# Expert pairs written out four times instead of looped; token positions moved from VectorE to GpSimd

## What is computed

```python
logits = h @ w_router
top_val, top_idx = lax.top_k(logits, 2)
top_w = jax.nn.softmax(top_val)
for e in range(8):
    out = out + gates[..., e:e + 1] * (silu(h @ w_gate[e]) * (h @ w_up[e])) @ w_down[e]
```

## Time and profile before

| | |
|---|---|
| median of 3 runs (lowest, highest) | 1273.4 us (1270.49, 1274.1) |
| the profiled execution's own time | 1276.08 us |
| its span in the trace | 1274.2 us |
| mean granted TensorE clock | 0.985 of full |
| TensorE busy | 1221.2 us, 96% of the span |
| VectorE busy | 689.5 us, 54% |
| ScalarE busy | 539.2 us, 42% |
| GpSimd busy | 106.9 us, 8% |
| DMA | 412.58 MB, mean 324 GB/s |

### The profile page before, as it was taken

The page is one execution under the profiler, slowest core; times in us unless marked ns, Lnnn a source line. Parts: engine busy times, 40 slices in busy tenths (PEclk is TensorE's granted clock), DMA queues, the critical chain, the costliest instruction groups (busy, mean ns, idle before and its releaser), DMA issues.

```text
span 1274.2 us, 16146 instructions
## 1 busy us (share of the span) xinstructions
PE 1221.2 (96%) x6044; PEld 854.6 (67%) x6044; DVE 689.5 (54%) x783; ACT 539.2 (42%) x522; POOL 106.9 (8%) x118
## 2 busy tenths in 40 slices
PE   9999999989989999998899999889999988999996
PEld 7888887778877888334688833568883346888332
DVE  3844445656578888102688710268861026886102
ACT  2643444455445776002577500257750025775001
POOL 0000000000003050100005010000501000050100
PEclk8999999999999999999999999999999999999998
DMA  9755553853266999999999999999999999999995
GB/s 314 257 187 178 196 178 120 199 188 131 100 248 225 372 363 360 347 409 414 413 415 406 368 371 408 415 414 415 407 346 386 407 415 414 415 406 341 391 407 209
DMA packets 141294, 412.58 MB, mean 324 GB/s; under 512 B 9683, under 2 KB 29139, under 8 KB 141142
## 3 DMA queue, kind: packets, MB, share of 16 engines
q1 hardware_dynamic: 140406, 408.23, 84.5%
q0 software_dynamic: 816, 3.28, 0.8%
HBM read 410.44 MB, written 1.05 MB: 323 GB/s over the span
## 4 chain that ended last, share of the span: by engine, by line
PE 85%; DMA 5%; DVE 3%; SPq 3%; issue 3%; ACT 1%; DVEq 0%; ACTq 0%
PE bank L1395 19%; PE bank L1396 19%; PE bank L1397 19%; PE bank L1768 13%; DMA raw<-in_moe_w_gate 4%; PE bank L1781 4%; SPq L545 3%; PE bank L1721 1%; PE bank L1402 1%; PE bank L1844 1%; PE bank L1491 1%; PE bank L1798 1%; PE bank L1657 1%; DMA head_row<-in_heads 1%; ACT w_hi L604 1%
## 5 line engine op out<-in xcount | busy, mean ns | idle before, releaser
L906 DVE TENSOR_TENSOR raw_lo<-raw,w_hi 128x2048 fp32r<-128x2048 f32 x149 | 339.8, 2300 | 101.4 <-ACT w_hi L604 101.2
L604 ACT ACTIVATE w_hi<-raw 128x2048 fp32r<-128x2048 f32 x149 | 284.5, 1916 | 148.3 <-PE bank L1397 95.7
L1395 PE MATMUL bank<-w_hi,h_hi 128*128 128x512 f32 x568 | 230.2, 405 | 19.4 <-DVE h_lo L1249 9.8
L1396 PE MATMUL bank<-raw_lo,h_hi 128*128 128x512 f32 x576 | 229.9, 399 | 9.1 <-issue 9.1
L1397 PE MATMUL bank<-w_hi,h_lo 128*128 128x512 f32 x568 | 226.5, 399 | 0.0
L1395 PEld LDWEIGHTS bank<-w_hi,h_hi 128*128 128x128 f32 x568 | 109.6, 193 | 50.2 <-DVE raw_lo L906 17.2
L1768 PE MATMUL bank<-raw,h_b 128*64 128x512 f32 (+1 forms) x768 | 143.1, 524 | 0.0
L1396 PEld LDWEIGHTS bank<-raw_lo,h_hi 128*128 128x128 f32 x576 | 111.1, 193 | 33.1 <-issue 10.4
L1397 PEld LDWEIGHTS bank<-w_hi,h_lo 128*128 128x128 f32 x568 | 109.2, 192 | 23.9
L906 DVE TENSOR_TENSOR raw_extra_lo<-raw_extra,w_hi 128x2048 fp32r<-128x2048 f32 x48 | 111.4, 2348 | 15.4 <-ACT w_hi L604 15.4
L1768 PEld LDWEIGHTS bank<-raw,h_b 128*64 128x64 f32 x768 | 53.7, 137 | 82.6 <-issue 74.5
(11 more groups left out here) (311 smaller groups left out, 1601.9 us busy)
## 6 DMA issues: line engine op xcount, KB each, us to landing
raw<-in_moe_w_gate SPq DMA_DIRECT2D x96, 1024.0 KB, 11.4
raw<-in_moe_w_up SPq DMA_DIRECT2D x80, 1024.0 KB, 11.8
raw<-in_moe_w_down SPq DMA_DIRECT2D x64, 1024.0 KB, 12.6
raw_extra<-in_moe_w_down SPq DMA_DIRECT2D x48, 1024.0 KB, 13.9
raw_extra<-in_moe_w_up SPq DMA_DIRECT2D x32, 1024.0 KB, 12.7
raw_extra<-in_moe_w_gate SPq DMA_DIRECT2D x16, 1024.0 KB, 7.4
raw<-in_ffn_w_gate SPq DMA_DIRECT2D x11, 1024.0 KB, 5.1
raw<-in_ffn_w_up SPq DMA_DIRECT2D x11, 1024.0 KB, 5.1
```

The lines of the kernel that those rows point to most:

```text
L604: nc.scalar.activation(to, raw_slot(source), ACT.Copy).then_inc(hi_ready, 1)
L906: nc.vector.tensor_tensor(lo_slot(source), raw_slot(source), high.bitcast(f32), ALU.subtract).then_inc(lo_ready, 1)
L1395: mm(out, a_hi, b_hi, start=first, stop=False)
L1396: mm(out, a_hi, b_lo, start=False, stop=False)
```

## The change

`pair(p)` is the old body as a function on ScalarE, VectorE and TensorE. It is called with the plain numbers 0 to 3, and then once more inside `Fori(PAIRS, pairs)` behind an `If`. With a plain number, waits have plain counts, and the two `If(p < pairs - 1)` go away in the first three rounds. The load of the number of rounds moves to the fourth round. SP's and GpSimd's loops stay. The positions move to GpSimd as 13 instructions, `reduce_sum` as three additions; VectorE only copies `rank` out of PSUM. The tables of experts are made inside round one.

```diff
+def pair_follows(eng, p, pairs):
+    return nullcontext() if isinstance(p, int) and p < PAIRS - 1 else eng.If(pairs[0] > p + 1)
...
 # ScalarE; VectorE the same
-            sc.wait_ge(pairs_done, 1)
-            pairs = sc.value_load(rtab_i[0:1, 0:1], min_val=PAIRS, max_val=PAIRS + X_PAIRS)
-            with sc.Fori(0, pairs) as p:
+            pairs = [None]
+            def pair(p):
...
-                with sc.If(p < pairs - 1):
+                if is_pair(p, PAIRS - 1):
+                    sc.wait_ge(pairs_done, 1)
+                    pairs[0] = pair_count(sc, rtab_i)
+                with pair_follows(sc, p, pairs):
                     hi_e(ROUND_UNITS)
...
+            for p in range(PAIRS):
+                pair(p)
+            with sc.If(pairs[0] > PAIRS):
+                with sc.Fori(PAIRS, pairs[0]) as p:
+                    pair(p)
...
 # VectorE, ahead of round one
             he_lo(0, halves=[1])
+            nc.vector.tensor_copy(rank[:, :, :], rank_ps).then_inc(rank_copied, 1)
             lo(MOE_U0 + 2)
             lo(MOE_U0 + 3)
-            link(nc.vector.tensor_tensor(more, incl, big, ALU.subtract))
...
-            nc.vector.reduce_sum(gpos[:, :, :], prod[:, :, :, :], AX.X).then_inc(gpos_done, 1)
-            nc.vector.max(order[:, :], key)
...
+            def order_table():
+                nc.vector.max(order[:, :], key)
...
 # VectorE, inside pair(p)
                     aT_low(p * N_EG + (N_FG + 2 * s + 1))
+                    if is_pair(p, 0) and s == 0:
+                        order_table()
...
 # TensorE
-            pe.wait_ge(pairs_done, 1)
-            pairs = pe.value_load(rtab_i[0:1, 0:1], min_val=PAIRS, max_val=PAIRS + X_PAIRS)
-            with pe.Fori(0, pairs) as p:
+            pairs = [None]
+            def pair(p):
...
-                    if s == N_BG - 2:
-                        with pe.If(p > pairs - 2):
+                    if s == N_BG - 2 and pairs[0] is not None:
+                        with pe.If(pairs[0] < p + 2):
+                            old_sums()
...
+            for p in range(PAIRS):
+                pair(p)
+            with pe.If(pairs[0] > PAIRS):
+                with pe.Fori(PAIRS, pairs[0]) as p:
+                    pair(p)
...
 # GpSimd
-            po.wait_ge(gpos_done, 1)
+            po.wait_ge(pairs_done, 1)
+            nc.gpsimd.tensor_tensor(more, incl, big, ALU.subtract).then_inc(pool_step, 1)
+            po.wait_ge(pool_step, 1)
+            nc.gpsimd.tensor_scalar(shift, more, float(CAP + CAP_B), float(PAIRS * (CAP + CAP_B)), ALU.mult,
+                                    ALU.add).then_inc(pool_step, 1)
...
+            nc.gpsimd.tensor_tensor(gpos[:, :, :], prod[:, :, :, 0], prod[:, :, :, 1], ALU.add).then_inc(pool_step, 1)
+            po.wait_ge(pool_step, TABLE_STEPS)
```

More of the change, by code:

```diff
@@ L1 @@
-from contextlib import ExitStack
+from contextlib import ExitStack, nullcontext
 import numpy as np
@@ L53 @@
 LAST_YG = 10
-FIRST_STEPS = 9
+TABLE_STEPS = 13
+FIRST_STEPS = TABLE_STEPS + 9
 WHOLE_UNITS = 3
@@ L96, in select, with is_pair, pair_count @@
     return n
+def is_pair(p, n):
+    return isinstance(p, int) and p == n
+def pair_follows(eng, p, pairs):
+    return nullcontext() if isinstance(p, int) and p < PAIRS - 1 else eng.If(pairs[0] > p + 1)
+def pair_count(eng, rtab_i):
+    return eng.value_load(rtab_i[0:1, 0:1], min_val=PAIRS, max_val=PAIRS + X_PAIRS)
 def trunk(nc, x_d, norm_g, pool_w, pool_scale, w_in, b_f, w_out, ffn_gate, ffn_up, ffn_down,
@@ L301, in trunk @@
         pairs_done = sem("pairs_done")
-        gpos_done = sem("gpos_done")
+        rank_copied = sem("rank_copied")
         sel_done = sem("sel_done")
@@ L1278, in _ @@
[L1278 to L1285, removed]
@@ L1294, in _ @@
[L1294 to L1299, removed]
@@ L1301, in _ @@
-            ve.wait_ge(pairs_done, 1)
-            pairs = ve.value_load(rtab_i[0:1, 0:1], min_val=PAIRS, max_val=PAIRS + X_PAIRS)
-            with ve.Fori(0, pairs) as p:
+            def order_table():
+                nc.vector.max(order[:, :], key)
+                link(nc.vector.tensor_tensor(within[:, :, :], incl[0:1, None, :].to_broadcast([1, X_PAIRS, E]),
+                                             iota[0:1, 0:X_PAIRS, None].to_broadcast([1, X_PAIRS, E]), ALU.is_le))
+                nc.vector.max_index(order_i[:, :], order[:, :], key)
+                link(nc.vector.reduce_sum(rtab[:, :], within[:, :, :], AX.X))
+                nc.vector.tensor_copy(rtab_i[:, 1:1 + PAIRS], order_i[0:1, 0:PAIRS])
+                nc.vector.tensor_scalar(rtab_i[:, 1 + PAIRS:1 + PAIRS + X_PAIRS], rtab[:, :], float(E - 1), None, ALU.min)
+                nc.vector.tensor_copy(rtab_i[:, 1 + PAIRS + X_PAIRS:1 + 2 * PAIRS + X_PAIRS],
+                                      order_i[0:1, PAIRS:2 * PAIRS]).then_inc(rtab_done, 1)
@@ L1359, in _ @@
                     nc.vector.tensor_copy(aT_bs[s % 2][:, 0:n], bank[2][:, 0:n]).then_inc(aT_lo_done, 1)
-                with ve.If(p < pairs - 1):
+                if is_pair(p, PAIRS - 1):
+                    pairs[0] = pair_count(ve, rtab_i)
+                with pair_follows(ve, p, pairs):
                     lo_e(ROUND_UNITS)
@@ L1853, in act_transposed, with old_sums @@
                     step.then_inc(aT_psum, 1)
-                for s in range(N_BG - 1):
-                    if s == N_BG - 2:
-                        with pe.If(p > pairs - 2):
[L1858 to L1862, removed]
+                def old_sums():
+                    pe.wait_ge(gT_done, p * 2 + 2)
+                    for tb in range(TB):
+                        for half in range(2):
+                            cols = slice(half * HALF, (half + 1) * HALF)
+                            mm(last_out(tb, half), ident, y[:, tb, cols], start=True, stop=False)
+                if is_pair(p, PAIRS - 1):
+                    pe.wait_ge(pairs_done, 1)
+                    pairs[0] = pair_count(pe, rtab_i)
+                for s in range(N_BG - 1):
+                    if s == N_BG - 2 and pairs[0] is not None:
+                        with pe.If(pairs[0] < p + 2):
+                            old_sums()
                     pe.wait_ge(silu_done, q0 + (N_EG + s + 1))
@@ L1874, in _ @@
                 down_b(N_BG - 2, range(2, 4))
-                with pe.If(p < pairs - 1):
+                with pair_follows(pe, p, pairs):
                     gather(p * 2 + 4, CAP)
@@ L1888, in _ @@
                                start=True, stop=True).then_inc(sc_psum, 1)
-            pe.wait_ge(ye_act, pairs * 2)
-            pe.wait_ge(gT_done, pairs * 2)
+            for p in range(PAIRS):
+                pair(p)
+            with pe.If(pairs[0] > PAIRS):
+                with pe.Fori(PAIRS, pairs[0]) as p:
+                    pair(p)
+            pe.wait_ge(ye_act, pairs[0] * 2)
+            pe.wait_ge(gT_done, pairs[0] * 2)
             for tb in range(TB):
@@ L1915, in _ @@
             iota_a = consts[:, C_IOTA:C_IOTA + P]
-            po.wait_ge(gpos_done, 1)
+            base, cap, big, incl, more, shift, most = (ctab[:, i, :] for i in (4, 5, 6, 7, 8, 9, 10))
+            po.wait_ge(pairs_done, 1)
[3 more added lines that the diff above has]
+                                    ALU.add).then_inc(pool_step, 1)
@@ new lines, in _ @@
+            nc.gpsimd.tensor_tensor(most, cap, base, ALU.add).then_inc(pool_step, 1)
+            po.wait_ge(pool_step, 3)
+            nc.gpsimd.tensor_tensor(shift, shift, most, ALU.subtract).then_inc(pool_step, 1)
+            po.wait_ge(rank_copied, 1)
+            nc.gpsimd.tensor_tensor(over[:, :, :], rank[:, :, :], cap[:, None, :].to_broadcast([P, TB, E]),
+                                    ALU.subtract).then_inc(pool_step, 1)
+            po.wait_ge(pool_step, 5)
+            nc.gpsimd.tensor_scalar(over[:, :, :], over[:, :, :], 0.0, None, ALU.is_ge).then_inc(pool_step, 1)
@@ new lines, in _ @@
+            nc.gpsimd.tensor_tensor(rank[:, :, :], rank[:, :, :], base[:, None, :].to_broadcast([P, TB, E]),
+                                    ALU.add).then_inc(pool_step, 1)
+            po.wait_ge(pool_step, 7)
+            nc.gpsimd.tensor_tensor(over[:, :, :], over[:, :, :], shift[:, None, :].to_broadcast([P, TB, E]),
+                                    ALU.mult).then_inc(pool_step, 1)
+            po.wait_ge(pool_step, 8)
+            nc.gpsimd.tensor_tensor(rank[:, :, :], rank[:, :, :], over[:, :, :], ALU.add).then_inc(pool_step, 1)
@@ new lines, in _ @@
+            po.wait_ge(pool_step, 9)
+            nc.gpsimd.tensor_tensor(prod[:, :, :, :], m12[:, :, :, :],
+                                    rank[:, :, None, :].to_broadcast([P, TB, 2, E]), ALU.mult).then_inc(pool_step, 1)
+            po.wait_ge(pool_step, 10)
+            nc.gpsimd.tensor_tensor(prod[:, :, :, 0:4], prod[:, :, :, 0:4], prod[:, :, :, 4:8],
+                                    ALU.add).then_inc(pool_step, 1)
+            po.wait_ge(pool_step, 11)
```

(2 more changed lines are left out.)

22 lines of the change are left out of this document (9 added, 13 removed).

## The result

Median 1254.1 us (1251.84 to 1259.77, 4 runs) against 1272.7 us before (4 runs): ratio 0.9862, interval 0.9826 to 0.9898, 17.6 us (13.0 to 22.1). The forecast, 20.9 us less, lies between them. The profiled execution took 1253.6 us with a span of 1251.8, 22.4 us less than before's span.

A forecast was written before the change was run, and what follows sets the result against it. TensorE, busy 96%, was taken as the bound, DMA close behind. Terms 4.0 + 18.0 - 0.6 - 0.5 = 20.9 us took the profiled 1276.08 us to 1255.2, the median to 1252.5; 8-in-10 range 1247 to 1263.

The forecast's parts named there:

- Jump back: Three round boundaries: without TensorE's jump, pauses and a half-clock stretch go; 6.0 us each, 18.0 us in all.
- two issue pauses: TensorE's gaps at each boundary, 2.14 and 2.92 us, put down to code fetched behind the jump; forecast to go.
- `h_lo` pause: TensorE's wait at each boundary, put down to late DMA; forecast to stay at 3.3 us with its half-clock stretch.
- Start: Start of round one: with VectorE's tables gone, TensorE's remainder wait and a half-clock stretch go; 4.0 us gained.
- DMA: All rounds: DMA is close behind TensorE and may not yield its whole slack; 0.5 us charged over three rounds.
- slack of 6.6 us a round: DMA's unused time in round two, 4.7 and 1.9 us; TensorE may lose that much before DMA sets the pace.
- the rival: Boundaries: only half of DMA's slack usable, 3.3 us gained each, the rest returning behind `h_lo`; 1260 us, chance 0.16.
- The sign that I named for DMA: In the changed profile, `h_lo` waits growing by several us would show the prediction wrong because of DMA.
- End: Kernel end: a new jump over the unused loop, 2.6 us covered, costs 0.6 us; bounds 0 to 3.4.
- Positions on GpSimd: Round one: 23 GpSimd instructions at 1.5 us make `gsel` ready near 424 us, 28 us of cover; priced nothing.
- slower rival: Round one: GpSimd at 4.68 us an instruction delivers `gsel` late, TensorE stands 43 us; 1296 us, chance 0.04.
- Register arithmetic: Waits with worked-out counts: 0.04 us extra each, hidden by TensorE's sequencer lead; 0, at most 1 us gained.

The follow-up runs named there:

- e1: The kernel before with only TensorE's rounds written out, ScalarE and VectorE still looped; ratio 0.9858 to the kernel before.
- e0_after: The changed kernel timed again beside the kernel before, with no edit; ratio 0.9812.
- e3: The changed kernel with the fourth gate unit's remainder made ahead of the four additions; ratio 0.9824 to the kernel before.
- e2: The changed kernel with TensorE and ScalarE looped as before; ratio 0.9958 to the kernel before.
- e10: The changed kernel with six TensorE jumps added, over 32, 192 and 768 products at the boundaries and 768 in part A; 1264.9 us, one run.
- e11: The changed kernel with TensorE jumps added at the three boundaries only, over 80, 128 and 320 products; 1258.5 us, one run.

## Why the prediction held, step by step

**Jump back.** The mechanism held: e1 shows that TensorE's loop alone makes the rounds shorter. The term was a little small: 6.0 us forecast for a boundary, 6.6 and 7.0 measured for the two whole rounds, about 20 us for three. The two issue pauses went and 1.04 us came, where 1.1 was forecast. Mis-sized was the half clock. I left the stretch behind the `h_lo` pause in all three boundaries; the changed kernel's first profile and e0_after have one such stretch at the boundaries, at the first, e3 has all three. A pause of 3.1 to 3.8 us there is sometimes followed by 3.41 us at half clock and sometimes not. That the term came out near its forecast all the same has another reason than the sum gives: once TensorE was fast enough, DMA set the round at 214.7 to 214.9 us, with a half-clock stretch and without.

Two readings in the prediction are off, and nothing hangs on them. The packets of the earlier trace rows move at 609.5 to 610 and 615.0 to 615.5 us, 2.4 to 2.9 us ahead of TensorE's next product and not 1 to 2. The forecast's own lower bound is 1252.5 - 3.3 = 1249.2 us, where 1248 was written.

**Why ScalarE's jump is cheap.** The prediction called its body short. The records of one of its rounds are 160, VectorE's 167, and their loops turn in 0.05 and 0.06 us; on TensorE a jump over 160 instructions cost 6.0. So length alone does not tell the engines apart, and what does is open.

**Start.** Forecast 4.0; the profiles show 4.5 and 4.0 (e0_after, above). e2, which has this part, VectorE's rounds written out and the positions on GpSimd, gained 5.4 (interval 2.7 to 8.0).

**DMA.** The slack of 6.6 us a round was read rightly and was used up: DMA moves 411 and 412 GB/s through both whole rounds, and a further 1 us saved for TensorE (e3) came back as waits. I charged 0.5 us over three rounds, and the rival gave DMA half of the slack; neither loss came, for all of the slack could be reached. The sign that I named for DMA, `h_lo` waits that grow by several us, did not come either, though DMA does set the round now: they went from 9.8 to 9.3 and 9.7 us, and to 10.6 in e3.

**End.** 0.6 us forecast. The jump took 3.37 us against a cover of 2.6, and the wait ahead of the last products grew from 0.7 to 1.3 us. The argument for it, empty queues and so nearer to 0, was wrong in part: most of the price stays with DMA idle.

**Positions on GpSimd.** Forecast ready near 424 us; 417.7 in fact, with 34 us of cover. The slower rival, GpSimd late, is refuted by the row above. Some of VectorE's remainders beside it took 2.52 us instead of 2.29, which no wait of TensorE shows.

**Register arithmetic.** Nothing, as forecast: e1's rounds are as long as the changed kernel's.

**The size.** Forecast 20.9 us, measured 17.6 and 24.0 by the medians and 25 by the profiles from the same mark on. Of the 25, 4.5 are the start, 6.6 and 7.0 the two whole rounds, and 7.1 the stretch from the third `h_lo` wait to the end (1044.35 to 1274.2 before, 1029.05 to 1251.8 after), with the 0.6 us of the end in it. The forecast had 16.9 for the last three together, so it is low by some 4 us there. The first profile's 2.8 us lost ahead of the rounds hide most of that in its own time. How much the other executions lost there is not shown, so that the medians came out on either side of the forecast is in part luck.

**What stays open.** Why the loop of before had a second pause in the third unit and the added forward jumps none; from where between 64 and 160 instructions a target is far, and whether distance or the place in the code decides; why the jump at the end costs 4.8 us in e10 and e11; whether a jump back with DMA idle costs what a forward one does.

## What to carry to other kernels

A loop on TensorE with a body like this one (about 2,000 instructions) pays about 6 us for each turn while weights stream. Forward jumps over 160 instructions and more pay the same, and 3.4 to 4.8 us with DMA idle. Write such a loop out where the count is sure, and let the sequencer run ahead of its array where it must stay. Before counting what a saved pause brings, take the idle share of DMA for the same round: here 6.6 us of slack carried 6.6 and 7.0 us of savings, and the next microsecond was worth 0.2 at most. Compare rounds between two marks inside the kernel as well as medians: the rounds agreed within 0.2 us where medians were uncertain by 3. Move small bookkeeping off the engine that feeds TensorE at the start of a stage, to one with tens of microseconds to spare.

## What the runs showed of the hardware

With DMA full, a jump of TensorE over 160 instructions costs as much as one over 1536 (6.0 us), and one over 64 a third of a microsecond. The price falls to 4.5 us where loads land in 5 to 6 us, and is 3.4 to 4.8 with DMA nearly idle. ScalarE's loop, whose body has some 160 records in a round, turns in 0.05 us. The granted clock of TensorE fell to half (1.2 GHz) for 3.41 us behind some pauses of about 3 us and not behind others. Such stretches ahead of the rounds moved one kernel's span by 5 us between two executions; in its two whole rounds they made no difference beyond 0.2 us, because DMA set the pace there.
